# RWKV scan on one Trainium2 core: VectorE inverts the first pair's blocks, GpSimd the others in three batches beside the scan, and GpSimd clears the scan's buffers

## What is computed

```python
def step(s, inp):
    rt, wt, kt, vt, kkt, at = inp
    sa = jnp.einsum('bhvk,bhk->bhv', s, -kkt)
    s = s * wt[:, :, None, :] + sa[..., None] * (kkt * at)[:, :, None, :] + vt[..., None] * kt[:, :, None, :]
    return s, jnp.einsum('bhvk,bhk->bhv', s, rt)
```

## Time and profile before

| | |
|---|---|
| median of three runs | 3784.49 us (3779.83 to 3784.79) |
| the profiled execution | 3781.54 us |
| its span in the trace | 3779.7 us |
| busy: PE, PE weight loads | 3473.6 us (92%), 3208.7 us (85%) |
| busy: DVE, ACT, POOL | 2045.8 us (54%), 1332.4 us (35%), 1295.5 us (34%) |

### The profile page before, as it was taken

The page is one execution under the profiler, slowest core; times in us unless marked ns, Lnnn a source line. Parts: engine busy times, 40 slices in busy tenths (PEclk is TensorE's granted clock), DMA queues, the critical chain, the costliest instruction groups (busy, mean ns, idle before and its releaser), DMA issues.

```text
span 3779.7 us, 67539 instructions
## 1 busy us (share of the span) xinstructions
PE 3473.6 (92%) x25106; PEld 3208.7 (85%) x25106; DVE 2045.8 (54%) x3535; ACT 1332.4 (35%) x2292; POOL 1295.5 (34%) x577
## 2 busy tenths in 40 slices
PE   6899999999999988974599999899999899999998
PEld 3789999998999977962488888799998776899997
DVE  7643774664266558478677676444754554331113
ACT  3343224415422255375232333343224323442223
POOL 0454334635633344301400000464335310464334
PEclk9999999999999999985799999999999999999999
DMA  7544554424455433466111111344544310343223
GB/s 268 157 127 149 195 186 142 131 83 122 133 173 176 149 107 119 143 205 217 52 56 59 43 56 35 112 127 155 185 151 134 98 34 1 101 134 95 72 72 119
DMA packets 174099, 460.36 MB, mean 122 GB/s; under 512 B 56864, under 2 KB 66528, under 8 KB 173152
## 3 DMA queue, kind: packets, MB, share of 16 engines
q1 hardware_dynamic: 145408, 438.46, 36.6%
q10 hardware_dynamic: 28512, 19.45, 1.6%
HBM read 419.41 MB, written 38.44 MB: 121 GB/s over the span
## 4 chain that ended last, share of the span: by engine, by line
issue 73%; POOL 16%; PE 6%; POOLq 2%; ACT 2%; DMA 1%; DVE 0%; ACTq 0%; DVEq 0%; SPq 0%
POOL ws L714 16%; PE banks L787 2%; PE banks L808 1%; PE banks L792 1%; POOLq L750 1%; POOLq L745 1%; PE banks L1117 1%; PE banks L818 0%; POOLq L722 0%; PE banks L1087 0%; PE banks L1140 0%; DMA inv_a<-blk_d 0%; ACT bt L2007 0%; DMA l<-in_l 0%; ACT L1997 0%
## 5 line engine op out<-in xcount | busy, mean ns | idle before, releaser
L714 POOL TENSOR_TENSOR ws<-wr,ws 128x1024 fp32r<-128x1024 f32 x509 | 1240.1, 2437 | 2309.6 <-ACT ws L1550 2309.3
L1550 ACT ACTIVATE ws<-wr 128x1024 fp32r<-128x1024 f32 x509 | 538.2, 1057 | 1053.6 <-PE banks L792 441.2
L787 PE MATMUL banks<-hs,ws 128*128 128x320 f32 x3712 | 564.3, 309 | 0.3 <-DVE hs L2678 0.3
L787 PEld LDWEIGHTS banks<-hs,ws 128*128 128x128 f32 x3712 | 549.3, 188 | 1.2 <-DVE hs L2678 0.9
L808 PE MATMUL banks<-hs,ws 128*128 128x320 f32 (+2 forms) x2624 | 444.9, 320 | 43.4 <-DVE hs L2316 13.7
L808 PEld LDWEIGHTS banks<-hs,ws 128*128 128x128 f32 x2624 | 403.3, 193 | 71.6 <-issue 26.2
L808 PE MATMUL banks<-fs,ws 128*128 128x320 f32 x2304 | 374.2, 312 | 12.9 <-DVE fs L3075 6.8
L2457 DVE SCALAR_TENSOR_TENSOR mjunk<-mr,banks 128x1024 f32<-128x1024 f32 x284 | 335.6, 1219 | 71.7 <-DMA mr<-in_m_slabs 48.4
L808 PEld LDWEIGHTS banks<-fs,ws 128*128 128x128 f32 x2304 | 344.1, 188 | 31.3 <-issue 12.7
L787 PE MATMUL banks<-fs,ws 128*128 128x320 f32 x2304 | 350.1, 309 | 0.0
L787 PEld LDWEIGHTS banks<-fs,ws 128*128 128x128 f32 x2304 | 340.7, 188 | 1.9 <-issue 1.9
(11 more groups left out here) (328 smaller groups left out, 4536.4 us busy)
## 6 DMA issues: line engine op xcount, KB each, us to landing
wr<-in_w_slabs SPq DMA_DIRECT2D x509, 512.0 KB, 3.6
mr<-in_m_slabs SPq DMA_DIRECT2D x167, 512.0 KB, 5.0
ar_d<-ar SPq DMA_DIRECT2D x16, 640.0 KB, 3.8
bk_d<-bt SPq DMA_DIRECT2D x16, 640.0 KB, 5.2
ar<-ar_d SPq DMA_DIRECT2D x16, 640.0 KB, 4.0
bk<-bk_d SPq DMA_DIRECT2D x16, 640.0 KB, 5.3
mx<-in_m_slabs SPq DMA_DIRECT2D x16, 512.0 KB, 6.6
rkv<-rkv_d SPq DMA_DIRECT2D x24, 320.0 KB, 5.2
```

Of the source, the lines that this page charges most:

```text
L714: pool.tensor_tensor(ws[s % 2][:, 1, :], wr[:, s % 2, :], ws[s % 2][:, 0, :].bitcast(F32), ALU.subtract).then_inc(lo_ready, 1)
L787: pe.matmul(pu[:, t % 2, h, 0:HT], ws[s % 2][:, 0, k * P:(k + 1) * P], src[:, k, part, h * HT:(h + 1) * HT], start=(k + part == 0), stop=F ...
L1550: act.activation(ws[s % 2][:, 0, :], wr[:, s % 2, :], ACT.Copy).then_inc(hi_ready, 1)
```

## The change

The 640 blocks are inverted in four parts, by the new table `INV_PAIRS` (first pair, end, blocks to a partition):

```diff
-INV_N = 5
-INV_G = 2
-INV_V = INV_N - INV_G
+INV_PAIRS = ((0, 1, 1), (1, 4, 2), (4, 7, 2), (7, KD, 1))
```

Pair 0 (80 partitions, one block each) is VectorE's, in two banks of PSUM; its blocks are loaded in the preparation, when SyncE comes to pair 2. Pairs 1 to 3 and 4 to 6 (120 partitions, two blocks each) and pair 7 (80 partitions, one) are GpSimd's, one after the other in the same buffers. SyncE's part:

```diff
                 for m in range(KD):
-                    if m == KD - 1:
-                        load_inverse(0, P - P // KD)
+                    if m == 2:
+                        load_blocks(0, 1)
...
-                load_inverse(P - P // KD, P)
...
                 load_operands(0, 1)
+                load_blocks(1, KD)
...
+                store_inverse(0)
+                sp.wait_ge(x_inv_stored, 16)
                 for d in range(2):
                     load_inverted(0, d)
-                with sp.Fori(0, KD - 1) as m:
+                for m in range(KD - 1):
                     sp.wait_ge(vrev_ready, m + 1)
                     sp.dma_start(vd[:, :], rkv_d[m + 1, 2]).then_inc(v_landed, 16)
                     sp.wait_ge(y_done, 2 * m + 1)
                     load_operands(m + 1, 0)
+                    if m < 3:
+                        store_inverse(m + 1)
+                        if m < 2:
+                            load_blocks(m + 2, KD)
+                        sp.wait_ge(x_inv_stored, 16 * (m + 2))
                     load_inverted(m + 1, 0)
```

GpSimd:

```diff
             low_parts(0, taken)
-            invert_part()
+            pool.wait_ge(prep_ready, 2 * KD)
+            pool.memset(at_[:, :, :, :, :], 0.0)
+            pool.memset(dt_[:, :, :], 0.0)
+            pool.wait_ge(blk_stored[0], 16 * KD)
+            pool.memset(sb_[:, :, :], 0.0).then_inc(zeroed, 1)
+            for i in range(1, 4):
+                invert(i)
             low_parts(taken, n_slabs)
```

`invert(i)` has the instructions of `invert_part` on the batch's partitions, behind `inv_landed` of its blocks and, from the second batch on, `x_inv_stored` of the batch before. TensorE, ScalarE and VectorE:

```diff
-                pe.wait_ge(inv_copied, INV_V)
+                pe.wait_ge(inv_copied, 1)
...
-                for q in range(INV_V):
-                    act.activation(inv_x[1][:, q, :, :], inv_p[:, q, :, :], ACT.Copy).then_inc(inv_copied, 1)
+                act.activation(inv_x[0][0:16 * NW, 0, :, :], inv_p[0:16 * NW, :, :], ACT.Copy).then_inc(inv_copied, 1)
...
-                for landed in inv_landed:
-                    dve.wait_ge(landed, 16)
+                dve.wait_ge(inv_landed, 16)
                 for j in range(31):
...
-                dve.memset(at_[:, :, :, :, :], 0.0)
-                dve.memset(sb_[:, :, :], 0.0)
-                dve.memset(dt_[:, :, :], 0.0)
-                dve.drain()
+                dve.wait_ge(zeroed, 1)
```

More of the change, by code:

```diff
@@ L726, in low_parts, with invert @@
                     low_part(s1 - 1)
-            def invert_part():
-                x, t = inv_x[0][:, :, :, :], inv_t[0]
-                for stored in ab_stored:
-                    pool.wait_ge(stored, 32 * (KD - 1))
-                pool.wait_ge(inv_landed[0], 16)
+            def invert(i):
+                m0, m1, q = INV_PAIRS[i]
+                n = 16 * NW * (m1 - m0) // q
+                x, t, blocks_in = inv_x[1][0:n, 0:q, :, :], inv_t[1][0:n, :], inv_a[1][0:n, 0:q, :, :]
+                pool.wait_ge(inv_landed, 16 * (i + 1))
+                if i > 1:
+                    pool.wait_ge(x_inv_stored, 16 * i)
                 pool.memset(x, 0.0)
```

89 lines of the change are left out of this document (45 added, 44 removed).

## The result

| | before | changed |
|---|---|---|
| median | 3784.47 us (3779.83 to 3784.79, 4 runs) | 3746.43 us (3741.89 to 3755.56, 4 runs) |
| profiled execution, its span | 3781.54, 3779.7 us | 3741.89, 3740.1 us |

The ratio is 0.9907, 95% interval 0.9889 to 0.9924: faster by 35 us, between 29 and 42 (the two medians lie 38 us apart). 3743.0 had been forecast, with 3734 to 3759 as range.

A forecast was written before the change was run, and what follows sets the result against it. The inversion was taken to bound the seam, TensorE the scan with VectorE close behind. 44.8 + 2.2 - 4.5 - 1.4 - 2.5 = 38.6 us off 3781.5 gave 3742.9, say 3743 us, range 3734 to 3759.

The forecast's parts named there:

- VectorE's inversion: At the seam: 62 instructions on one block per partition instead of three take 26.4 us instead of 48.7.
- TensorE's start: At the seam: TensorE starts at 1791.4 instead of 1830.25 and transposes at 1802.2 instead of 1847.02, 44.8 us gained.
- They cost nothing: VectorE's three clearings, moved to GpSimd, end near 1768, needed at 1793; without that cover they would cost 6 us once.
- clock term: Pair 0's first 20 products: 2.39 us instead of 4.63 at the low clock, 2.2 us gained.
- first batch: GpSimd's first batch of inverses: pair 1's `xc` lands at 1855 to 1857, ahead of 1858.6, no wait, 2 us spare.
- Collisions in pair 1: VectorE's two-input instructions and casts beside GpSimd in pair 1: 4.5 us lost, bounds 0 and 9.6.
- second batch: GpSimd's second batch, its store ahead of pair 2's `xc` in SyncE's order: `xc` lands at 1931, 1.4 us lost.
- Pair 2: VectorE's collisions in pair 2 beside the shorter instructions of GpSimd's third batch: 2.5 us lost, bounds 0 and 5.
- C: Rival: every VectorE instruction shuts GpSimd out; slower from batches of 84.5 us on, 3802 us at 95; 5%.
- A: Rival: GpSimd paces the first two pairs; batches of 70 us give 3752.5, of 76 us 3764.5; 19%.
- B: Rival: hardly any collision in the scan, both batches in time; 46 to 47 us gained, 3735; 12%.
- D: Rival: TensorE's start stays where it was because another semaphore comes last; nothing moves, 3781 us; 2%.

The follow-up runs named there:

- number 4: The changed kernel with the three buffer clearings moved back to VectorE, behind its inversion: 3746.89 us, ratio 0.9907.
- number 1: The changed kernel measured again without any edit: 3750.16 us, ratio 0.9925.
- 8: The changed kernel with pair 0 inverted in SBUF and GpSimd's batches regrouped as pair 1, pairs 2 to 4, pairs 5 to 7: 3753.04 us, ratio 0.992.
- number 9: The changed kernel with GpSimd standing still during `finish` of pairs 1 to 3 and batches 2 and 3 stored in pairs 2 and 3: 3740.79 us, ratio 0.9881.
- number 6: The changed kernel with memsets for product and sum in GpSimd's batches 2 and 3, inverses of pairs 4 to 7 left out: 3745.63 us, ratio 0.9899.
- second: The second measurement of the changed kernel, without any edit: 3750.16 us, ratio 0.9925.
- third measurement: The changed kernel measured a third time without any edit: 3751.25 us, ratio 0.9910.
- run 3: Not a label: in "a profiled run 3 us under that median" it is the profiled execution of the kernel before the change, 3781.54 us.
- number 7: The changed kernel with other batches on GpSimd: pair 1 alone, pairs 2 to 4, pairs 5 to 7: 3754.16 us, ratio 0.9922.
- number 10: The kernel of number 9 with 24 TensorE products that nobody reads, ahead of the first triangle: 3737.42 us, ratio 0.9873.
- 11: The kernel of number 9 with 32 TensorE products that nobody reads, ahead of the first triangle: 3746.54 us, ratio 0.9901.

## Why the prediction was nearly right

- **VectorE's inversion**: 26.4 us forecast, 26.0 measured. Fixed cost and cost per element from two rows carried over to a third of the size.
- **TensorE's start**, forecast 29.7 us behind the end of preparation (1791.4 - 1761.7), came at 28.9; the transposes, forecast at 40.5, at 40.88. So of 44.8 us 44.4 came. "They cost nothing" held for the clearings. What they would cost without that cover was put at 6 us and was 3.4 at the seam (number 4), since the first triangles cover a part, and nothing in the whole.
- **The clock term failed**: 2.2 us forecast, 0.55 got. The reason given was that TensorE "no longer sits 8 us before the first products". It still sits 3.44 us, and the first 20 products took 3.37 us, between the 4.63 and the 2.39 of the earlier trace rows. In numbers 1, 8 and 9, behind the same 3.44 us, the clock stayed up and pair 0's first direction took 30.9 us instead of the 33.16 before, the 2.2 us that were forecast; no run shows what decides it. In number 1 and number 9 the gain went at once into the wait for pair 1's `xc`.
- **The first batch**: it was to have 2 us to spare and had 0.29 in this trace and none in others (a wait of 1.18 us in number 1), which the prediction names as a sign of being wrong. The batch itself came as counted (62.3 us); its store took 6.5 us to land where 3.9 had been put, with the load of blocks issued just behind it.
- **Collisions in pair 1**: 4.5 forecast, 4.68 measured, gone when GpSimd is idle (number 9) and down to 0.45 when it only writes (number 6). The kind was right, the agreement is luck: VectorE lost 3.06 us there, a third less than forecast, and the other 1.6 are TensorE's products at the 1.2 GHz level behind the wait, for which the prediction has no term. With other batches the same direction costs 7.3.
- **The second batch was the largest miss**: 1.4 us forecast, 4.69 measured. The blocks arrived 98.3 us behind the end of preparation instead of 93.3, because the load took 10.3 us, beside the store that was issued 0.4 us ahead of it. GpSimd's batch gave 3.7 of that back (65.6 us with its clearing, where 69.3 had been counted, 5 of them for collisions that cost it 1.3). The second store and `xc`, put at 3.9 and 2.8 us, took 9.6 together, again with a load beside them; and VectorE came for `xc` 2.3 us later than counted, from what it lost before. 1.4 + 5.0 - 3.7 + 3.0 - 2.3 = 3.4, VectorE's 3.31. The step from there to TensorE was missing altogether: TensorE stands 3.21 us with both buffers full (until 1933.56), and then makes the next triangles at the 1.2 GHz level, so that VectorE waits 1.49 us for the fourth where it waited 0.18 before. 3.31 and 1.3 are the direction's 4.69 to within 0.1.
- **Pair 2**: 2.5 forecast, 2.54 measured, and luck again. The lengthened instructions (two scalings, `ecm`, L2834) come to 0.9 us; the other 1.63 are the 40 products, 6.26 us instead of 4.63. In number 1, where the clock stayed up, the direction lost 0.86 us.
- **The sum**: 38.6 forecast, 33.1 measured, the difference 1.65 from the clock at the first products and 3.3 from the second batch, with 0.4 and 0.2 from seam and pair 1. That the median agreed within 3.4 us is luck as well: 33.1 us under the median of before would be 3751.4, which is where the second and third measurement lie (3750 and 3751), while the forecast started from a profiled run 3 us under that median and the first measurement came out 5 us lower than this.
- **What the terms have in common**: of the 11.9 us lost beside the scan some 4.6 are the clock behind waits of 2 to 4 us. The prediction counted waits at their own length only. Its collision terms were too large by 3 us, 7.0 against 4.0.
- **The rivals**: GpSimd's batches took 62 to 63 us, far from 84.5 (C) and from 70 (A), although the wait that A describes exists. B falls with the 12 us lost, D with TensorE's wait of 27.77 us.

## What to carry to other kernels

Work that is moved to an idle engine is free only where neither its ports nor a queue in program order meets the chain that the bound engine waits for. Here 12 of 45 us went back through six short instructions and one store, and through TensorE's clock behind the waits that they made. Three waits on an existing semaphore, which make the idle engine stand still while that chain runs, and stores placed later, returned 10 to 12 of them. Place a store beside the first consumer that needs it. That it should also not share the DMA engines with a load that has time is a guess from the landing times; no run kept the two apart. Before costing a transfer, look at what goes out in the same microsecond.

## What was not expected of the hardware

- GpSimd instructions that only write left VectorE's two-input instructions at 0.83 and 0.88 us; those that read lengthened them to as much as 1.75. The loss was what GpSimd's instruction had left when VectorE's began, less 0.13 to 0.20 us: up to 0.7 us each in the changed kernel (0.49 to 1.19, 0.82 to 1.47), and 0.9 in number 7 (0.83 to 1.75), where 1.07 us of a sum of 1.19 were left.
- GpSimd is held up as well: a sum of 120x504 that took 1.17 us on average in number 9 took 1.57 beside `finish` in number 7.
- A wait of 3.31 us on VectorE became 4.69 us on TensorE, since the wait let TensorE's granted clock fall to 0.50, and the triangles behind it came late as well.
- Behind nearly the same wait for `zz`, 2.06 and 2.02 us, the granted clock fell to 0.50 in the first trace of the changed kernel and stayed at 1.00 in the second, 1.7 us of difference in one direction.
- TensorE's granted clock was 1.00 before and 0.50 behind 3.86 us of idleness in number 10, and needless products ahead of the seam didn't pay in numbers 10 and 11.
